# Softmax attention of a two-layer hybrid block: the slice of the background gate job moved from behind a step's transpositions to between its values and its transpositions

## The reference, cut to what matters

```
q, k, v = project(p_lat, True);  qc, kc, vc = project(p_ctx, False)
s = einsum(q_block, keys) * scale          # 128 queries, up to 768 keys
p = softmax(s)                             # B: window of 3 blocks + context + sink
o = einsum(p, values)
...
gates = sigmoid(gate_logits)               # gate_logits = h @ w_in[gate columns]
x = x + mod * (sum over mixers of gates * (o @ w_branch)) @ w_o
```

## Time and profile before

| | |
|---|---|
| median of three runs | 3240.27 us (3240.13 to 3242.03) |
| profiled execution, its time | 3240.14 us |
| its span, first to last instruction | 3238.5 us |
| PE busy | 3002.2 us, 93% |
| DVE, ACT, POOL busy | 1429.0, 1182.3 and 158.5 us |
| mean granted TensorE clock | 0.973 |

### The profile page before, as it was taken

One profiled execution on the slowest core, in us unless ns is written; L12 is line 12 of the kernel. 1 busy time (PEld: TensorE's weight loads), 2 busy tenths in 40 slices (PEclk: granted clock), 3 DMA queues, 4 the chain that ended last, 5 costly groups with the idle time before them and its releaser, 6 DMA issues.

```text
span 3238.5 us, 39370 instructions
## 1 busy us (share of the span) xinstructions
PE 3002.2 (93%) x15968; PEld 2359.0 (73%) x15968; DVE 1429.0 (44%) x2312; ACT 1182.3 (37%) x2047; POOL 158.5 (5%) x179
## 2 busy tenths in 40 slices
PE   6988899999999999999999989889998899889998
PEld 4877785577668677788888868767457666678886
DVE  4266642335443444423233342764335544454444
ACT  4343333334543432412121244443334544442222
POOL 0022210000000000000000000211000000000000
PEclk8999999999999999999999989999999999999999
DMA  5222240031212132333333322224012031323332
GB/s 192 66 91 90 84 136 30 20 103 64 69 70 80 62 120 73 90 106 105 102 101 104 98 80 68 79 75 140 8 52 76 23 108 33 120 81 96 97 98 91
DMA packets 83758, 273.78 MB, mean 85 GB/s; under 512 B 9345, under 2 KB 9601, under 8 KB 82689
## 3 DMA queue, kind: packets, MB, share of 16 engines
q1 hardware_dynamic: 74896, 229.84, 21.9%
q0 software_dynamic: 8688, 41.49, 3.8%
HBM read 245.07 MB, written 26.21 MB: 84 GB/s over the span
## 4 chain that ended last, share of the span: by engine, by line
PE 83%; DVE 6%; ACT 5%; issue 3%; DMA 2%; SPq 0%; DVEq 0%; ACTq 0%
PE slot L625 81%; PE slot L1030 2%; DVE rowmax L1902 1%; ACT SS L1449 1%; DMA SS<-g_kept 1%; ACT tmp L1224 1%; DVE wl L1560 1%; ACT PT_B L1435 1%; ACT wh L1133 0%; ACT Hh L1226 0%; DVE Yl L1925 0%; DVE XS L1779 0%; PE slot L795 0%; DMA X<-xT_dram 0%; DMA g_kept<-logits_out 0%
## 5 line engine op out<-in xcount | busy, mean ns | idle before, releaser
L625 PE MATMUL slot<-Hh,wh 128*128 128x512 f32 (+1 forms) x2368 | 872.5, 370 | 36.1 <-DVE Hl L1607 14.1
L625 PE MATMUL slot<-Hl,wh 128*128 128x512 f32 (+1 forms) x2368 | 836.1, 354 | 0.0
L625 PE MATMUL slot<-Hh,wl 128*128 128x512 f32 (+1 forms) x2368 | 835.9, 354 | 0.0
L625 PEld LDWEIGHTS slot<-Hh,wh 128*128 128x128 f32 x2368 | 451.5, 191 | 113.4 <-issue 28.9
L625 PEld LDWEIGHTS slot<-Hh,wl 128*128 128x128 f32 x2368 | 450.8, 191 | 62.7
L625 PEld LDWEIGHTS slot<-Hl,wh 128*128 128x128 f32 x2368 | 452.4, 192 | 59.3 <-issue 5.8
L1560 DVE TENSOR_TENSOR wl<-raw,wh 128x1024 fp32r<-128x1024 f32 (+1 forms) x208 | 227.7, 1095 | 271.2 <-ACT wh L1133 268.3
L625 PE MATMUL slot<-Uh,wh 128*128 128x512 f32 (+1 forms) x768 | 274.7, 358 | 0.0
L625 PE MATMUL slot<-Ul,wh 128*128 128x512 f32 (+1 forms) x768 | 272.3, 355 | 0.0
L625 PE MATMUL slot<-Uh,wl 128*128 128x512 f32 (+1 forms) x768 | 271.9, 354 | 0.0
L1133 ACT ACTIVATE wh<-raw 128x1024 fp32r<-128x1024 f32 (+1 forms) x208 | 192.4, 925 | 189.5 <-PE slot L625 157.7
(11 more groups left out here) (238 smaller groups left out, 4145.8 us busy)
## 6 DMA issues: line engine op xcount, KB each, us to landing
raw<-w_dram SPq DMA_DIRECT2D x204, 512.0 KB, 3.6
raw<-w_gate_dram SPq DMA_DIRECT2D x64, 512.0 KB, 3.6
ada_g_raw<-ada_dram POOLq DMA_DIRECT2D x48, 512.0 KB, 3.9
ada_g_raw<-ada_dram SPq DMA_DIRECT2D x32, 512.0 KB, 3.8
raw<-w_merge_dram SPq DMA_DIRECT2D x64, 256.0 KB, 2.7
g_kept<-logits_out SPq DMA_DIRECT2D x32, 384.0 KB, 2.3
SS<-g_kept SPq DMA_DIRECT2D x32, 384.0 KB, 3.3
ada_first<-ada_dram SPq DMA_DIRECT2D x8, 1024.0 KB, 18.2
```

Source lines behind the costliest of these rows:

```text
L625: return pe.matmul(dst, lhsT, rhs, start=start, stop=stop)
```

## The change

In `attention` of the tensor engine's stream, the slice of the background job is issued between the values and the transpositions of a step instead of behind the transpositions. Nothing is added or removed, and the streams of the other engines are the same.

```diff
@@ attention(branch, layer), tensor engine
                         last.then_inc(o_done.sem, 1)
+                    if i < len(tiles):
+                        for step in steps[i]:
+                            later_gate(layer, FIRST_GATE[layer][branch] + step[0], *step[1:])
                     if LAG <= i < len(tiles) + LAG:
 
                         tile = tiles[i - LAG]
...
                             units += 1
                             values_in += 1
-                    if i < len(tiles):
-                        for step in steps[i]:
-                            later_gate(layer, FIRST_GATE[layer][branch] + step[0], *step[1:])
                 chain_over(("c0", "c1", ("unit", 0), ("unit", 1), "values"))
```

## The result

The changed kernel takes 3253.35 us (median of 16 runs, 3244.57 to 3261.31) against 3241.15 us for the kernel before (16 runs, 3232.67 to 3255.99). The ratio is 1.0033 with a 95% interval of 1.002 to 1.0046, so +10.7 us, between 6.5 and 14.9. That is the difference of the means, 10.8; the medians differ by 12.2. It is slower; the forecast was 3246.1, and 3253.35 lies above the range of 3240 to 3251. Single runs of one kernel lie up to 15 us from its median, more than the effect, so what follows reads the loops of the traces and not the totals.

What follows compares the result with a forecast made beforehand. TensorE, busy 3002.2 of 3238.5 us, was taken as the bound, so its waits count. Late part starts, shorter transposition waits and loop tails summed to +5.9 us on 3240.14, forecast 3246.1, range 3240 to 3251.

Steps and rivals of the forecast that it cites:

- (a): Where a gate part starts, its first slice waits for ScalarE's copy of the part before, with less cover: +7.7 us.
- six single starts in layer 0's B: Part starts standing alone, steps 4, 10, 22, 28, 34, 46: 0.24 to 0.47 us each by key blocks, +2.1 us.
- the two pairs: Layer 0's B, part starts close together on context tiles, steps 16 and 18, 40 and 42: +2.25 us.
- (b): Transpositions wait less for copies of transposed probabilities, in the two B loops only: -4.5 of 18.7 us.
- (c): Last steps of the six loops: two transpositions stand together with no slice between to cover the copy, +2.65 us.
- Rival 1: VectorE's and ScalarE's chain holds every values product, so shorter transposition waits gain nothing: 3250.5 us, chance 0.2.
- rival 2: Part starts are hidden after all, ScalarE's logits copy ending while scores run: 3239 to 3243 us, chance 0.2.
- rival 3: ScalarE copies transpositions at once, so all 18.7 us of waits go and starts are covered: 3224 us, chance 0.06.
- the signs named for the changed profile: Transposition waits fall to about 5 us, waits on `logits_out` and `mod` rise some 5, and loop lengths shift as listed.
- the high bound of (a): Each of 12 exposed part starts costs a whole six-block transposition and its wait, 0.72 us: some 11 us.
- The sentence on the clock: A clock fall costs about 1.6 us near split products, nothing visible when f32 values products meet it, as at 870.
- Rival 4: Two or more clock falls appear or vanish near split products, 3.2 us each way: 3249 or 3243, chance 0.04.

Runs made afterwards that it cites:

- the two repeats: The kernel before and the changed kernel, each profiled once more with nothing altered: 3244.11 and 3257.6 us.
- x6_b1: Kernel before with the new order in layer 1's B alone, save its last step: 3241.07 us against 3248.26, ratio 0.9986.
- x3_rest: Kernel before with the new order at all steps but part starts and each loop's last step: ratio 0.9988 to the kernel before.
- x2_last: Kernel before with the new order only at the last step of each loop: ratio 1.0008 to the kernel before.
- x1_starts: Kernel before with the new order only at steps whose slice starts a part of a gate job: 3255.13 us against 3246.22, ratio 1.0039.
- x4_act_first: The full change, plus ScalarE copying a finished gate part before the transposed units: ratio 1.0011 to the kernel before.
- r_before: The kernel before, run once more with nothing altered: 3244.11 us.

## Why the prediction was right and where it failed

The sum by its own terms, measured on segments that no fall of the clock touches, or between executions that have the same fall in them (the two repeats, for the first segments):

| term | forecast | measured |
|---|---|---|
| (a) six single starts in layer 0's B | +2.1 | +3.0 (0.2, 0.59, 0.59, 0.43, 0.59, 0.59) |
| (a) the two pairs | +2.25 | +3.6 (1.61 and 2.02) |
| (a) layer 0's D | +2.8 | +2.8 (0.63, 0.73, 0.73, 0.75) |
| (a) layer 0's A | +0.55 | +0.25 (+0.46 behind the first values product, -0.21 before it) |
| (b) layer 0's B | -1.6 | -1.5 (0.76 and 0.75) |
| (b) layer 1's B | -2.9 | -3.1 |
| (c) the tails | +2.65 | +2.8 |
| layer 1's A, beside its tail | 0 | +0.5 |
| sum | +5.9 | +8.3 |

**(b) and (c) were right in size and place.** Of 18.7 us of waits only a quarter came back, since VectorE's and ScalarE's chain holds most values products, as the earlier trace rows had shown; x6_b1 and x3_rest confirm where it does not, and x2_last the tails. Rival 1 is out by x6_b1, rival 2 by x1_starts, rival 3 by the 14.3 us for which the values products still wait. Of the signs named for the changed profile, line 1033's waits came to 6.2 (forecast about 5); those on `logits_out` and `mod` rose more than forecast, by 10.1 and 5.8 us where about 5 together was said; layer 0's B is 5.1 us longer and not 3.2, D 3.3 (3.4), A 0.6 (1.2); layer 1's B is 2.5 shorter at equal falls (2.5), A 0.9 and not 0.3 longer, D 0.5 (0.3).

**The step that failed is (a): its main mechanism was right, its size in layer 0's B was not, and a wait was missing from it.** The prediction took 7.7 us, and 9.7 were measured. Three errors make it up. At single starts I had the copies of T(i-1) "stay" where they were against the scores; they come 0.2 us later (before, copies at 806.98 and the last scores matmul at 807.33; after, 808.84 and 809.00), so the slice waits 0.68 us behind the scores and not 0.49. Behind context tiles I priced the start by the time of a two-block transposition (0.24), and the loss was 0.59 at steps 22 and 46. x1_starts has 0.54 there with the starts alone, so it belongs to the start and not to its neighbours. Some 0.2 of it is gone when the next scores start; the rest is lost at the values product behind them, which waits 0.23 us for the copy of the transposition that the slice now holds up and waited for nothing before. I had no term for that wait. x4_act_first bears it out: the slice is freed there and the wait of that product stays. At the pairs I carried only the starts through. Alone they cost 1.15 and 1.58 us (x1_starts), 0.2 and 0.3 more than my 0.95 and 1.3; but the steps between them, 17 and 19, lose another 0.51 and 0.68 by the new order (x3_rest), where I had counted nothing. The two sums, 1.66 and 2.26, are near the 1.61 and 2.02 of the full change. What the high bound of (a) allowed, some 11 us, was nearer than what I took, and steps that are not starts had no term at all; they also make the 0.5 us of layer 1's A (0.10 and 0.14 a group in x3_rest, 0.05 and 0 in x1_starts).

**The sentence on the clock was wrong.** It said that a fall met by the f32 values costs nothing. The trace of before has the counter-example in the very fall that the earlier trace rows show. The values product of a group of context tiles in layer 0's B, in the timeline of before, at a granted clock of 0.53 over its length:

```profile
869.92 3.63 PE L625 MATMUL slot<-PT_B,VB 128*64 128x512 f32 x4 [1.06 <-ACT PT_B L1435]
```

and the same product in the changed kernel, which has no fall there:

```profile
873.83 1.93 PE L625 MATMUL slot<-PT_B,VB 128*64 128x512 f32 x4 [1.06 <-ACT PT_B L1435]
```

It takes 1.7 us more, so these f32 matmuls do lose by a fall. The comparison of V(27) with V(7), from which I had it, set a group with two key blocks against one with four, and a fall against none. In layer 1's B both executions of the changed kernel have two falls that neither of the kernel before has inside the loop, one near V(15) (about 1.0 us by the segments, against x6_b1) and one at the last values product. In the changed kernel, and then in x6_b1:

```profile
2616.92 5.34 PE L625 MATMUL slot<-PT_B,VB 128*64 128x512 f32 x8 [0.64 <-ACT PT_B L1435]
```

```profile
2608.23 3.65 PE L625 MATMUL slot<-PT_B,VB 128*64 128x512 f32 x8 [0.64 <-ACT PT_B L1446]
```

That is 2.7 us, against which stand the 1.7 us of the fall in layer 0's B that both have lost. So +8.3 by the order and +1.0 by falls that both executions share make 9.3 of the 10.7 us (6.5 to 14.9) that the times show. That the order brings these falls is not shown: the kernel before has one that begins at the end of this loop and lies behind it, x1_starts has the one near V(15) and x4_act_first the one at the last values product, x3_rest and x6_b1 have neither. What is left of the 10.3 us of the first two profiles is mostly the longer fall at the start of layer 0's B, 1.4 us, which the second execution has not. The rest of the 10.7 lies within its interval, where falls come and go between executions; I can't assign it. Rival 4 priced such falls, but as an alternative to the sum and not on top of it.

## What to carry to other kernels

A job used as filler between dependent steps has two ends: moving it to cover one wait uncovers another, so price both at each place and move it only where the first is larger. Here that is one loop of six, with ScalarE's answer to the transpositions late, no short tiles, and a single copy at the start of a part; which of the three makes the difference was not tried. If the slice must be early, the copy that frees its bank has to be moved ahead in the queue of the other engine too: order on two engines is one decision. And a chain carried by hand should take in every step between two events, also those at which nothing is thought to happen, and every reader of what is moved: here the values product that waits for a late transposition.

## What the runs showed that I had not expected

The granted clock falls at different places, and for different lengths, in executions of the same code. The start of layer 0's A, the same 5 us in before and then in r_before (TensorE busy all of it, 20 matmuls against 7, at granted clocks of 1.00 and 0.50; the loops start at 542.7 and 545.0):

```profile
560.00:565.00 5.00, 5.00 (x20) 2.61 (x19) 2.01 (x7) 1.17 (x3) 0.00 (x0) 1.00 0.00 0
```

```profile
560.00:565.00 5.00, 5.00 (x7) 1.41 (x6) 0.14 (x1) 0.44 (x2) 0.00 (x0) 0.50 0.00 0
```

The first values product of that loop comes 37.9 us after the first scores in one and 44.4 in the other. The Trainium skill ("TensorE: Matmul & The Clock Gate", the section on HAM oscillation) ties such falls to idle gaps between groups of matmuls; its example has far longer waits than these loops. No run here shows that rule at work. The two falls inside layer 1's B come at the same steps in both executions of the changed kernel, but in a loop whose idle time is 13.9 us, against 16.6 in before and 14.0 in x6_b1, which have neither; and at the start of layer 0's A the same code gave a short fall in before and a long one in r_before. A single run of this kernel, with its scatter of up to 15 us, therefore tells nothing of an effect of this size; the segments of a loop that hold no fall tell 0.1 us.
